# A streaming-encoder trunk on one core: down weights in runs of 8 KB per partition, and the experts' weight units around one ring that takes in the high parts' buffers

## The reference

```python
def swiglu(h, w1, w3, w2):
    return (jax.nn.silu(h @ w1) * (h @ w3)) @ w2

def moe_swiglu(h, w_router, w1, w3, w2):
    xt = h.reshape(-1, d)
    logits = (xt @ w_router).astype(jnp.float32)
    top_val, top_idx = lax.top_k(logits, TOP_K)
    gate = jax.nn.softmax(top_val, axis=-1)
    combine = jnp.sum(jax.nn.one_hot(top_idx, N_EXPERTS) * gate[..., None], axis=1)
    for e in range(N_EXPERTS):
        y = y + combine[:, e:e + 1] * swiglu(xt, w1[e], w3[e], w2[e])
```

## Time and profile before

| | us |
|---|---|
| median of 3 runs | 1205.4 |
| lowest and highest | 1204.85, 1206.19 |
| the profiled execution, its device time | 1205.0 |
| its span in the profile | 1203.1 |
| PE busy in it | 1132.7 |
| DVE, ACT, POOL busy in it | 300.4, 200.3, 41.6 |
| moved by DMA in it | 418.11 MB |

### The profile page before, as it was taken

How to read it: one execution, slowest core, us unless ns; L and a number is a source line. 1 busy time by engine, 2 the same in 40 slices (tenths; PEclk the granted TensorE clock), 3 DMA queues, 4 the chain that set the end, 5 groups by cost and what they waited for, 6 DMA issues and landing times.

```text
span 1203.1 us, 26594 instructions
## 1 busy us (share of the span) xinstructions
PE 1132.7 (94%) x12278; PEld 615.0 (51%) x12278; DVE 300.4 (25%) x408; ACT 200.3 (17%) x284; POOL 41.6 (3%) x37
## 2 busy tenths in 40 slices
PE   7999999999999999979999999977799999999775
PEld 6888888889753354333345335412333543363122
DVE  4654545468661011201110101111011111011002
ACT  5444334456630000000000000000000000000002
POOL 3000000011000000000000000000000000000000
PEclk9999999999999999999999999999999999999998
DMA  9975556513489999999999999999999999999994
GB/s 346 388 267 186 199 178 203 178 62 123 146 322 395 389 415 413 412 411 418 416 410 414 418 415 408 418 416 412 413 418 415 407 417 418 401 405 419 419 404 186
DMA packets 97865, 418.11 MB, mean 348 GB/s; under 512 B 8515, under 2 KB 14709, under 8 KB 97749
## 3 DMA queue, kind: packets, MB, share of 16 engines
q1 hardware_dynamic: 94288, 410.06, 86.5%
q0 software_dynamic: 1488, 4.59, 1.0%
q10 hardware_dynamic: 1972, 1.70, 0.4%
HBM read 414.23 MB, written 2.10 MB: 346 GB/s over the span
## 4 chain that ended last, share of the span: by engine, by line
PE 73%; DMA 16%; SPq 9%; issue 1%; ACT 1%; DVE 0%; ACTq 0%; DVEq 0%
PE psum L757 33%; PE psum L782 11%; DMA up<-in_moe_w 9%; SPq L589 9%; PE psum L669 8%; PE psum L671 8%; PE psum L670 8%; DMA down<-in_moe_w 7%; PE psum L677 1%; PE psum L748 1%; PE psum L865 1%; PE psum L738 1%; DMA consts<-in_table 0%; PE psum L986 0%; PE psum L770 0%
## 5 line engine op out<-in xcount | busy, mean ns | idle before, releaser
L757 PE MATMUL psum<-up,xg 128*32 128x448 f32 x5328 | 514.3, 540 | 27.2 <-DMA up<-in_moe_w 27.1
L757 PEld LDWEIGHTS psum<-up,xg 128*32 128x32 f32 x5328 | 167.9, 110 | 365.1 <-issue 300.6
L782 PE MATMUL psum<-down,hid_t 128*32 128x256 f32 x4704 | 263.4, 380 | 24.6 <-DMA down<-in_moe_w 24.4
L782 PEld LDWEIGHTS psum<-down,hid_t 128*32 128x32 f32 x4704 | 149.4, 110 | 140.1 <-DMA down<-in_moe_w 39.0
L1439 DVE TENSOR_TENSOR low<-raw,high 128x2048 fp32r<-128x2048 f32 x50 | 114.6, 2291 | 85.5 <-ACT high L1148 85.3
L1559 DVE TENSOR_TENSOR sil<-sil,psum 128x1344 f32<-128x1344 f32 (+1 forms) x16 | 22.1, 1379 | 438.1 <-PE psum L757 438.1
L1148 ACT ACTIVATE high<-raw 128x2048 fp32r<-128x2048 f32 x51 | 97.8, 1917 | 82.0 <-PE psum L671 81.2
L669 PE MATMUL psum<-high,a_hi 128*128 128x512 f32 x224 | 87.3, 390 | 0.9 <-DVE a_lo L1476 0.9
L671 PE MATMUL psum<-low,a_hi 128*128 128x512 f32 x224 | 87.1, 389 | 0.0
L670 PE MATMUL psum<-high,a_lo 128*128 128x512 f32 x224 | 87.1, 389 | 0.0
L1212 ACT ACTIVATE sil<-psum 128x1344 f32<-128x1344 f32 (+1 forms) x16 | 18.4, 1151 | 395.0 <-PE psum L757 395.0
(11 more groups left out here) (241 smaller groups left out, 643.3 us busy)
## 6 DMA issues: line engine op xcount, KB each, us to landing
up<-in_moe_w SPq DMA_DIRECT2D x256, 896.0 KB, 23.7
down<-in_moe_w SPq DMA_DIRECT2D x112, 1024.0 KB, 18.7
raw<-in_ffn_w SPq DMA_DIRECT2D x42, 1024.0 KB, 6.7
raw<-in_w_q SPq DMA_DIRECT2D x4, 1024.0 KB, 5.1
raw<-in_w_o SPq DMA_DIRECT2D x4, 1024.0 KB, 5.0
x_res<-in_x SPq DMA_DIRECT2D x2, 512.0 KB, 5.5
raw<-in_pool_w SPq DMA_DIRECT2D x1, 1024.0 KB, 11.0
raw<-in_w_kv SPq DMA_DIRECT2D x1, 1024.0 KB, 5.8
```

Source lines behind the costliest of these rows:

```text
L757: mm = pe.matmul(out3[g * BLK:(g + 1) * BLK, r, :], xg[:, k, r * BLK:(r + 1) * BLK], w[:, g], start=k == 0, stop=k == DT - 1)
L782: mm = pe.matmul(Y[g * BLK:(g + 1) * BLK, r, :], hid_t[:, c, r, b * BLK:(b + 1) * BLK], w[:, bb, g * GW:(g + 1) * GW], start=c == 0 and b ...
```

## The change

It has four parts.

1. **Down units in runs of 8 KB.** The view of w2 becomes `(i p b) f -> p i (b f)`: partition p takes the neighbouring rows 2p and 2p + 1 of the unit's 256 rows, which are one run of 8 KB in HBM, in place of rows p and 128 + p, two runs of 4 KB. The unit is the same 1 MB of HBM. So that the hidden values meet their rows, the columns of the up units are taken in runs of 64 words (`p (i g j) -> p g i j`), and DVE's turn into `hid_t` reads every second word of its source and writes its pieces at a stride.
2. **One ring.** In the first pass the experts' units go round a ring of `SPACE` = 17 x 2048 words, which is the 14 buffers and the three high buffers behind them. A unit starts where the last one ended, or at 0 if it would not fit. `round_the_ring` writes down each unit's place (`MOE_PLACES`) and the count that its load waits for (`MOE_FREED`).
3. **Buffers of units 0 to 52** are numbered by `(u - U_MOE) % RING`, so that unit 39 lies in buffer 0, 40 in buffer 1, and 52 in buffer 13.
4. **The second and third pass** keep the halves, and SP waits before them until the first pass has used all its units.

```diff
+SPACE = (RING + NHI) * UNIT
+def slot(u):
+    return (u - U_MOE) % RING
+def moe_size(j):
+    return UNIT if MOE_UNITS[j % MU][0] == "w2" else FC
+def round_the_ring():
+    user = [0] * (SPACE // GRAIN)
+    def take(start, size, u):
+        grains = slice(start // GRAIN, (start + size) // GRAIN)
+        before = max(user[grains])
+        user[grains] = [u] * (size // GRAIN)
+        return before + 1
+    for u in range(U_MOE):
+        take(slot(u) * UNIT, UNIT, u)
+        if u >= U_DENSE:
+            take((RING + hslot(u)) * UNIT, UNIT, u)
+    places, freed, start = [], [], 0
+    for j in range(E * MU):
+        size = moe_size(j)
+        if start + size > SPACE:
+            start = 0
+        places.append(start)
+        freed.append(take(start, size, U_MOE + j))
+        start += size
+    return places, freed
...
-                   "w2": moe_w2.rearrange("o e (k p) f -> (o e) p k f", p=P)}
+                   "w2": moe_w2.rearrange("o e (i p b) f -> (o e) p i (b f)", p=P, b=2)}
...
-                part = experts[kind][bass.ds(e, 1), :, NF * c + 2 * i:NF * c + 2 * i + 2, :]
+                part = experts[kind][bass.ds(e, 1), :, NF // 2 * c + i:NF // 2 * c + i + 1, :]
...
-        def slot(u):
-            return u % RING
...
             with sp.If(again > 0):
+                sp.wait_ge(unit_used, U_MOE + E * MU)
...
-                w = up_w[MOE_HALF[kind, c]][k][:].rearrange("p (b g i) -> p g b i", g=4, i=BLK)
+                return weights[:, start:start + FC].rearrange("p (i g j) -> p g i j", g=4, j=2 * BLK)
...
-                    dve.transpose(hid_t[:, c, 0:nb], sil[:, 0:nb]).then_inc(hidden_lo, 1)
+                    dve.transpose(hid_t[:, c, 0:nb].rearrange("p r (i b m) -> p (r i) b m", b=2, m=BLK),
+                                  sil[:, 0:nb].rearrange("p r (i m b) -> p (r i) b m", b=2, m=BLK)
+                                  ).then_inc(hidden_lo, 1)
```

More of the change, by code:

```diff
@@ L83 @@
 HALF = RING * UNIT // 2
+SPACE = (RING + NHI) * UNIT
+GRAIN = 256
 SCATTER_AFTER = 2
@@ L118, in freed_by @@
     for back in range(1, 2 * MU):
[L119 to L123, removed]
+        s_, e_ = moe_place(j - back)
         if s_ < end and start < e_:
@@ L188, in trunk_program @@
         high = [at(f"high{r}", [P, UNIT], F32R, place(UNIT * 4)) for r in range(NHI)]
+        weights = at("weights", [P, SPACE], F32, o_raw)
         x_res = at("x_res", [P, NT, D], F32, place(8 * K))
@@ L432, in expert_source, with expert_tile @@
             return part.rearrange("o p k f -> p (o k) f")
-        def expert_tile(kind, c, i):
-            h = MOE_HALF[kind, c]
-            return down_w[h][i][:] if kind == "w2" else up_w[h][i][:].unsqueeze(1)
-        def slot(u):
-            return u % RING
+        def expert_tile(ps, j, e):
+            start = ps.place(j, e)
+            return weights[:, start:start + moe_size(j)].unsqueeze(1)
         def turn_bank(c, t):
             return banks[OUT[0][t] if c == 0 else UP1[t]]
-        def hslot(u):
-            return (u - U_DENSE) % NHI
         def turned_x(d):
@@ L490, in freed, with place @@
                 if isinstance(e, int):
-                    return freed_by((self.n0 + e) * MU + j)
+                    return MOE_FREED[e * MU + j]
                 return e * MU + freed_by(self.n0 * MU + j)
+            def place(self, j, e):
+                if isinstance(e, int):
+                    return MOE_PLACES[e * MU + j]
+                return moe_place(j)[0]
             def experts(self, n, e):
@@ L767, in expert_up_first @@
                         pe.wait_ge(moe_landed[k], PASSES[0].landed(k, 0))
-                        w = up_w[MOE_HALF["w1", 0]][k][:].rearrange("p (b g i) -> p g b i", g=4, i=BLK)
+                        w = up_weights(PASSES[0].place(k, 0))
                         for g in range(4):
@@ L773, in expert_up_first, with expert_down @@
                             mm.then_inc(unit_used, 1)
-            def expert_down(c, i, nb):
-                w = down_w[MOE_HALF["w2", c]][i]
+            def expert_down(start, c, i, nb):
+                w = weights[:, start:start + UNIT].rearrange("p (b n) -> p b n", b=2)
                 for bb in range(2):
@@ L825, in expert_feed_forward @@
                     if kind == "w2":
-                        mm = expert_down(c, i, ps.blocks(e))
+                        mm = expert_down(ps.place(j, e), c, i, ps.blocks(e))
                     else:
-                        mm = expert_up(kind, c, i, H1 if kind == "w1" else H3, ps.blocks(e))
+                        mm = expert_up(ps.place(j, e), i, H1 if kind == "w1" else H3, ps.blocks(e))
                     mm.then_inc(unit_used, 1)
@@ L855, in _ @@
             pe.wait_ge(pooled, DT // 2)
[L856 removed]
+            pe.wait_ge(landed[slot(U_POOLW)], 16)
             pe.wait_ge(gains_ready, 1)
```

25 lines of the change are left out of this document (14 added, 11 removed).

## The result

The changed kernel takes 1192.37 us (median of 4 runs, 1191.52 to 1193.17), against 1205.12 for the one before beside it. The ratio is 0.9895, 95% interval 0.9877 to 0.9912: 12.6 us less, between 10.6 and 14.8. Forecast were 1191.1 us and 14.3 us less.

A forecast was written before the change was run, and what follows sets the result against it. PE was taken to bound expert 0 and DMA everything from expert 1 on. From the median 1205.4 us, 6.6 us for the ring and 7.7 us for 8 KB runs gave 1191.1 us, range 1186.0 to 1199.5.

The forecast's parts named there:

- Part 1, the ring: When expert 0 ends, loads are 19 units ahead, not 16; 2.75 MB leave the DMA-bound stretch, saving 6.6 us.
- Part 2, 8 KB runs: The 98 down units of experts 1 to 7 load at 420.4 GB/s instead of 407.5, saving 7.7 us.
- The line through 4 KB and 7 KB: Weight loads cost 9.8 ns a run plus 0.0369 ns a byte per engine; 311.8 ns for 8 KB.
- Part 3, the turn: DVE's turn into hid_t takes up to 3.2 us, hidden behind PE's other work: 0 us.
- rival C: Experts of 3 blocks stop DMA running ahead; four of seven give back 4.4 us of rate gain: 1195.5 us, chance 0.07.
- A: Ring gain only; 8 KB runs in down units move no faster: 1198.8 us, chance 0.09.
- B: Rate gain only; loads idle as long in expert 0, so 2.75 MB are not ahead: 1197.7 us, chance 0.03.
- D: Down units' 8 KB runs move slower a byte than 4 KB; at 377 GB/s 1219.2 us, chance 0.09.
- PE's first wait: PE's first wait for weights, taken to be near 490 us before, comes some 14 us later.
- The last landing: The last weights land near 1175.4 us instead of 1189.7, with 13.4 us of finish behind.

The follow-up runs named there:

- One_block: Changed kernel with PE multiplying only the first block of 32 tokens of every expert, all loads kept: 1180.78 us, ratio 0.9801 to the kernel before.
- ring_only: Changed kernel with down units again in runs of 4 KB, columns and turn as before, keeping the ring of 17 and new numbering: 1199.37 us, ratio 0.9955.
- head_start: ring_only with its ring cut to the 14 buffers, so first expert loads go earlier without more room: 1204.51 us, ratio 1.0004 to the kernel before.

## Why the prediction was right

**What bounds, and where.** Right: PE in expert 0, DMA from expert 1 on. One_block shows the first from the other side: without PE's pace expert 0 moves 420 GB/s.

**Part 1, the ring: 6.6 us.** 5.4 measured (3.9 to 7.0); the last weights of expert 0 landed 5.8 us earlier in ring_only and 5.5 us in the changed kernel. The reading that the room pays and the head start does not is shown by head_start (0) beside ring_only.

**Part 2, 8 KB runs: 7.7 us.** 6.1 measured (4.6 to 7.7). The line through 4 KB and 7 KB was right over the whole range: 85.3, 311.8 and 613.7 ns forecast, 86, 312 and 613 ns the median packet of 2, 8 and 16 KB. 387, 408 and 420 GB/s are the rates for 2, 4 and 8 KB. The Trainium skill ("DMA: Bandwidth & Descriptors", Specifications) puts runs of 4 KB at line rate already; these rates do not agree. What the term passed over is that 408 and 420 are means of sixteen engines and the end goes by the late eight. In experts 1 to 7 the early group took 10.9 us less for down units (254.6 to 243.7 us), part of which was, it seems, the queue's holding it back before; the late group took 6.5 us less for everything (758.2 to 751.7). So the term was 1.6 us too large, and the first one 1.2; both differences are within the intervals, and together 12.6 us were measured where 14.3 were forecast. Why the late group gained less than the line gives is not settled.

**Part 3, the turn: hidden.** Right. The turn, which I had put at up to 3.2 us in place of 1.6, takes 1.58 us for every second word and 2.50 for every 14th.

**PE as the bound (rival C).** Did not happen. PE runs through the pairs of 3-block experts without a wait, and DMA stays at 418 GB/s:

```profile
545.00:765.00 220.00, 220.00 (x2980) 96.26 (x2976) 27.87 (x42) 6.79 (x6) 4.73 (x5) 1.00 1.01 418
866.00:1085.00 219.00, 219.00 (x2979) 96.16 (x2976) 26.19 (x38) 6.79 (x6) 4.71 (x5) 1.00 1.01 418
```

**Rivals A and B** would have been 1198.8 and 1197.7 us; the kernels that do the one part alone took 1199.4 and 1198.2. **D**: 8 KB runs are not slower a byte, nor are 16 KB ones.

**Forecast but off.** PE's first wait came 12.2 us later and not 14, and it was at 513.6 us in the kernel before, not near 490: there SP waited for PE, as the chain above shows. The last landing came at 1177.8 us and not 1175.4. That eight engines fall behind the others, and that the end hangs on them, was not in the prediction at all; the terms were worked out from means over all sixteen, and that they hold so nearly for the late eight is in part luck.

## What to carry to other kernels

Where one stage is bound by compute and the next by DMA, bytes loaded ahead count only if the buffers can hold them until the first stage ends: more room was worth 5 us, an earlier start in the old room nothing. On a stream of loads the run per partition still counts at 4 KB (9.8 ns a run, 408 against 420 GB/s at 8 KB); but do not buy longer runs with coarser loads in a stage where loads wait for single buffers. And read the completions of single DMA engines, not the mean rate alone, before pricing a DMA-bound end: here the late eight were 10 to 17 us behind the first.

## What the runs showed of the hardware

- Loads over 128 partitions on sixteen engines: a run costs 9.8 ns and 0.0369 ns a byte on one engine. The line gives the median packet of 2, 4, 7, 8 and 16 KB (86, 161, 274, 312 and 613 ns) within 1 ns.
- What SP's queue held, as estimates from the median time to landing over the time of a unit: 11 up units with 8 runs per engine (24.1 us by 2.19), 10 down units with 8 (26.3 by 2.49), 7 with 16 (18.9 by 2.57), and 5 with 32 (14.5 by 2.73). More runs in a unit meant fewer units.
- Instruction fetches come as packets of 16 KB, 1.06 us each, and take an engine from the weights meanwhile. In the changed kernel eight of the sixteen engines fell back by some 2.0 us with every expert of 46 units ((16.8 - 2.9)/7), and by less than half of that where PE ran fewer instructions ((7.9 - 1.8)/7 = 0.9 in one_block).
- Splitting 28 of the 98 down loads of experts 1 to 7 into pieces of 112, 8 and 8 partitions took the stream from 419 to 269 GB/s while every engine was busy; 28 additional loads over 8 partitions cost 29 us.
